# Threshold search of a sparse attention layer: where the candidate less the next bit is formed

## What is computed

```python
raw = jnp.einsum('bqhe,ble->bqhl', qi, ki).astype(f32) * IDX_DIM ** -0.5
score = jnp.einsum('bqhl,bqh->bql', jax.nn.relu(raw), wi.astype(f32)) * N_IDX_HEADS ** -0.5
score = jnp.where(adm[None], score, -jnp.inf)
_, idx = lax.top_k(score, topk)
```

## Time and profile before

| | us |
|---|---|
| median of three runs | 2905.49 |
| the profiled execution, device time | 2906.05 |
| its span in the trace | 2904.3 |
| TensorE busy in the span | 2825.2 (97%) |
| VectorE busy | 1538.2 (53%) |
| ScalarE busy | 700.3 (24%) |
| GpSimd busy | 899.6 (31%) |
| the search, first count to last candidate | 1456 to 1607.6 |

### The profile page before, as it was taken

How to read it: one execution, slowest core, us unless ns; L and a number is a source line. 1 busy time by engine, 2 the same in 40 slices (tenths; PEclk the granted TensorE clock), 3 DMA queues, 4 the chain that set the end, 5 groups by cost and what they waited for, 6 DMA issues and landing times. The chain is left out here.

```text
span 2904.3 us, 47791 instructions
## 1 busy us (share of the span) xinstructions
PE 2825.2 (97%) x18337; PEld 2662.8 (92%) x18337; DVE 1538.2 (53%) x2822; ACT 700.3 (24%) x1441; POOL 899.6 (31%) x854
## 2 busy tenths in 40 slices
PE   7999999999999999999978999999999999999998
PEld 6987799999999999998578777789999999999997
DVE  6146616544544444455688878533644454444455
ACT  4037711000000000013467766631100000000002
POOL 2233332222222222224024754323222222222221
PEclk9999999999999999999999999999999999999999
DMA  4530011111111111114012000021111111111112
GB/s 125 69 97 11 21 37 37 44 36 43 36 36 43 43 43 43 36 44 133 1 32 78 11 11 10 21 76 43 44 37 43 43 42 37 43 43 36 43 37 76
DMA packets 178206, 129.79 MB, mean 45 GB/s; under 512 B 25313, under 2 KB 168353, under 8 KB 177846
## 3 DMA queue, kind: packets, MB, share of 16 engines
q1 hardware_dynamic: 178066, 127.90, 15.4%
HBM read 111.13 MB, written 15.16 MB: 43 GB/s over the span
## 5 line engine op out<-in xcount | busy, mean ns | idle before, releaser
L1237 POOL CAST w_hi<-w_raw 128x1024 fp32r<-128x1024 f32 x120 | 145.1, 1209 | 1098.9 <-PE ps_gemm L1474 600.2
L684 DVE TENSOR_TENSOR h<-h,ps_gemm 128x1170 f32<-128x1170 f32 (+1 forms) x192 | 262.5, 1367 | 371.8 <-PE ps_gemm L1490 208.5
L1474 PE MATMUL ps_gemm<-xh,w_hi 128*128 128x390 f32 (+1 forms) x1920 | 445.8, 340 | 0.0
L1474 PE MATMUL ps_gemm<-xl,w_hi 128*128 128x390 f32 (+1 forms) x1920 | 444.9, 340 | 0.0
L1474 PE MATMUL ps_gemm<-xh,w_lo 128*128 128x390 f32 (+1 forms) x1920 | 444.7, 340 | 0.0
L1474 PEld LDWEIGHTS ps_gemm<-xh,w_hi 128*128 128x128 f32 x1920 | 349.2, 189 | 0.1
L1474 PEld LDWEIGHTS ps_gemm<-xl,w_hi 128*128 128x128 f32 x1920 | 348.1, 189 | 0.0
L1474 PEld LDWEIGHTS ps_gemm<-xh,w_lo 128*128 128x128 f32 x1920 | 348.0, 189 | 0.0
L1240 POOL TENSOR_TENSOR w_lo<-w_raw,w_hi 128x1024 fp32r<-128x1024 f32 x120 | 289.4, 2411 | 17.4
L692 ACT ACTIVATE ac<-ac 128x1184 f32<-128x1184 f32 x44 | 52.5, 1194 | 858.0 <-DVE ac L751 858.0
L1435 PE MATMUL ps_gemm<-xl,w_hi 128*128 128x390 f32 (+1 forms) x1056 | 246.6, 342 | 0.0
(11 more groups left out here) (418 smaller groups left out, 4672.6 us busy)
## 6 DMA issues: line engine op xcount, KB each, us to landing
w_raw<-in_w_gate SPq DMA_DIRECT2D x44, 512.0 KB, 3.8
w_raw<-in_w_up SPq DMA_DIRECT2D x44, 512.0 KB, 3.8
w_raw<-in_w_down SPq DMA_DIRECT2D x44, 512.0 KB, 3.4
w_raw<-in_w_in_b SPq DMA_DIRECT2D x13, 512.0 KB, 4.0
w_raw<-in_w_qkv_a SPq DMA_DIRECT2D x10, 512.0 KB, 4.0
residual_park<-h SPq DMA_DIRECT2D x1, 4680.0 KB, 13.7
h<-residual_park SPq DMA_DIRECT2D x8, 585.0 KB, 7.9
out<-yt SPq DMA_DIRECT2D x9, 512.0 KB
```

The lines of the kernel that those rows point to most:

```text
L684: dve.tensor_tensor(c3(h[:, m, :], l), c3(h[:, m, :], l), pse(j, l), ALU.add).then_inc(evac[j % 2], 1)
L1237: pool.tensor_copy(whi[c % 3][:], raw[c % 2][:]).then_inc(w_hi_done, 1)
L1474: mm = pe.matmul(ps[j % 2][:, m_, 0:ch], w[:, k, :], x[:, k, x0 + m_ * ch:x0 + (m_ + 1) * ch], start=(k == 0 and w is wh and x is XH), sto ...
```

## The change

ScalarE forms `above` behind its three counts of each round of the two loops, as a copy with a constant bias, into seven columns of `small` in SBUF. VectorE's subtraction L2503 is gone. VectorE waits for ScalarE's `above` between the comparison and the new candidate. The other edits follow from that: a semaphore more, one bit value less to set, fewer search steps to number.

```diff
         cand_new = sem("candidate_ready")
+        above_done = sem("candidate_less_next_bit_done")
...
+        above = small[:, 14:21]
...
             for n, (kind, j, view) in enumerate(steps):
                 counts(view, CAND[kind] + j, COUNTS[kind] + j)
+                if kind in ABOVE:
+                    act.activation(above, candm, ACT.Copy, bias=-2.0 ** (TOP[kind] - j - 1)).then_inc(above_done, 1)
                 if n in after:
                     take_projection(after[n])
...
-            sign, pred, tmp, need, bv = F(0), F(35), F(43), F(50), F(57, 6)
-            kk, above, bits_made = tb[0][:, 0:7], tb[0][:, 8:15], F(21)
+            sign, pred, tmp, need, bv = F(0), F(35), F(43), F(50), F(57, 5)
+            kk, bits_made = tb[0][:, 0:7], F(21)
...
                         wait_at(dve, cand_new, CAND[kind] + j, unroll, i)
-                        dve.tensor_scalar(above, candm, bv[:, j + 1:j + 2], None, ALU.subtract).then_inc(srch, 1)
                         counts(view, COUNTS[kind] + j, i, unroll)
                         dve.tensor_tensor(pred, cnt, kk, ALU.is_le).then_inc(srch, 1)
-                        wait_at(dve, srch, base + 2 * j + 2, 2 * unroll + 1, i)
+                        wait_at(dve, above_done, ABOVE[kind] + j + 1, unroll, i)
+                        wait_at(dve, srch, base + j + 1, unroll + 1, i)
                         dve.scalar_tensor_tensor(candm, pred, bv[:, j:j + 1], above, ALU.mult, ALU.add).then_inc(cand_new, 1)
```

More of the change, by code:

```diff
@@ L869, in build @@
         COUNTS = {"sign": 0, "high": 1, "above": 1 + S1, "low": 2 + S1}
-        SRCH_OPS = 1 + 3 + 6 + 2 + (1 + 3 * 11) + 1 + 1 + 2 + (1 + 4 * 9) + 2 + 1
+        ABOVE = {"high": 0, "low": S1}
+        TOP = {"high": S1 - 1, "low": S2 - 1}
+        SRCH_OPS = 1 + 3 + 6 + 2 + (1 + 3 * 6) + 1 + 1 + 2 + (1 + 4 * 5) + 2 + 1
         MASK_STEPS = [(6, k) for k in (0, 2, 3, 4, 5, 6, 7)] + [(c, k) for c in range(6) for k in range(8)]
@@ L2492, in bits @@
             def bits(view, kind, top, rounds, unroll):
-                for k in range(unroll + 1):
+                for k in range(unroll):
                     ins = dve.memset(bv[:, k:k + 1], 2.0 ** (top - k))
@@ L2509, in bits @@
                     dve.scalar_tensor_tensor(bv, bv, 2.0 ** -unroll, bv, ALU.mult, ALU.bypass).then_inc(srch, 1)
-                    wait_at(dve, srch, base + 2 * unroll + 1, 2 * unroll + 1, i)
-                step[0] += rounds * (2 * unroll + 1)
+                    wait_at(dve, srch, base + unroll + 1, unroll + 1, i)
+                step[0] += rounds * (unroll + 1)
                 dve.wait_ge(cand_new, CAND[kind] + rounds * unroll)
             flip(-1.0)
-            bits(high_half, "high", 14, 3, 5)
+            bits(high_half, "high", TOP["high"], 3, 5)
             high = F(0 + 43)
@@ L2526, in _ @@
             done(dve.tensor_tensor(kk, kk, cnt, ALU.subtract))
-            bits(low_kept, "low", 15, 4, 4)
+            bits(low_kept, "low", TOP["low"], 4, 4)
             done(dve.tensor_copy(bits_made.bitcast(I16)[:, 1::2], high))
```

## The result

The changed kernel took 2916.79 us (median of 6 runs, 2914.94 to 2921.59), the kernel before 2906.68 in the same comparison: ratio 1.0035, 95% interval 1.0025 to 1.0045, or about +10.2 us. It is slower, as forecast for 2912.2, but by more, and 0.8 us above the range's upper end. The profiled execution of after has a span of 2915.9 us.

The account below looks back on a forecast made before the run. TensorE's two long waits for the search were taken to bound the kernel. Saving -2.7 and ScalarE's operation +1.3 gave -1.4; with port +8.2 that made +6.8, taken as +6.7: 2912.2 us, range 2903.8 to 2916.0.

Parts of the forecast that it names:

- What bounds the kernel: TensorE, busy nearly always, waits twice for the search; the time changes by the sum of both waits' changes.
- the two waits: TensorE's two longest waits, inside the search: 15.3 and 18.6 us instead of 12.8 and 14.4.
- The port term: Candidates and `bv` updates with two SBUF operands wait for GpSimd: 3.0 and 5.2 us, sum +8.2.
- n = 18: That round's candidate misses GpSimd's second product by 0.2 us and doesn't wait; later by that, 2.2 us.
- n = 24: Its candidate misses GpSimd's second product by 0.2 us; the `bv` update behind it waits 2.1, before 1.9.
- The short ones: Candidates n = 5, 14 and 28 wait 0.4 us for GpSimd's cast; n = 9 waits 0.4 for a product.
- The saving: Without VectorE's subtraction an ordinary round saves 0.15 us: 1.2 before the kv copy, 1.5 behind job 8, together -2.7.
- ScalarE's operation: The new copy takes 0.18 us, hidden in rounds without a projection, 0.09 of the queue otherwise; sum +1.3 us.
- rival 3: Candidates n = 18 and 24 fall into GpSimd's second product, +2.2 us each: some 2916 us, chance 0.13.

Follow-up runs that it names:

- e6: The changed kernel without VectorE's wait for `cnt_done` ahead of the first two counts of a round: 2914.58 us, ratio 1.0019.
- e13: e3 without the `cnt_done` wait ahead of a round's first two counts, and with ScalarE's new operation issued twice: 2907.93 us, ratio 1.0006.
- e3: The changed kernel with the comparison's outcome in PSUM instead of SBUF: 2907.62 us, ratio 1.000.
- e2: The kernel before, VectorE still subtracting but writing `above` to SBUF instead of PSUM: 2923.10 us, ratio 1.0049.
- e8: The kernel before with the unread second input of the `bv` update in PSUM instead of SBUF: 2907.41 us, ratio 1.000.
- e11: e3 with the `cnt_done` wait ahead of the first two counts of a round written twice: 2913.78 us, ratio 1.002.
- e5: The kernel before without VectorE's wait for `cnt_done` ahead of the first two counts of a round: 2910.26 us, ratio 1.0005.

## Why the prediction was wrong, step by step

- **What bounds the kernel: right.** The time follows the two waits, 9.6 us against a measured 10.2 (7.3 to 13.1 by the interval).
- **The port term: right in kind and place, and nearly in size.** Before the kv copy 2.3 us (0.05 + 2.21 + 0.07 over the undisturbed durations) for 3.0; behind job 8, without n = 18, 4.6 us (0.22 + 1.87 + 0.16 + 0.17 + 2.14, of which the update behind n = 24 counts only by what it added) for 5.2. The short ones came out shorter because the candidates, having saved less, came later and met less of the cast. In e6, where they come earlier, the same ones take 0.54 (n = 5), 0.54 (n = 14) and 0.47 us (n = 28).
- **The saving: the term that was mis-sized.** The prediction took 0.05 us for a wait directly behind another, from the nearest gap, with 0 and 0.20 as bounds. It is 0.14 (e6 against after): 0.07 for the wait, and 0.07 for the register instruction in front of it, which the prediction did not count in an ordinary round. Of the 0.20 us between the subtraction and the first count, 0.16 stayed. A round saves 0.04 us in the high half and nothing in the low half, where a register instruction more stands ahead of the wait for `above`. Instead of -2.7 us the saving is some -0.3.
- **ScalarE's operation: right.** 0.194 us for 0.18, and 0.09 in the queue for 0.09 (e13). Since rounds stayed at 3.77, most of the +1.3 us wasn't paid. Saving and operation together were forecast at -1.4 us and are +0.7 in the waits of e3 (13.1 and 14.8).
- **n = 18: the step that failed.** The prediction put it clear of GpSimd's second product by 0.2 us and wrote that later by that it would wait 2.2. ScalarE starts its counts of n = 17 at a = 1547.44 in after. The product begins at a + 7.41, as forecast (7.4). But the candidates n = 17 and 18 come at a + 3.67 and a + 7.49 instead of 3.4 and 7.2. So n = 18 waited 2.1 us more. In e6 (a = 1546.99) they come at a + 3.50 and a + 7.31, and n = 18 gets by: the register instruction and the wait ahead of the first count make 0.17 to 0.18 of the 0.29 us, enough to decide it. That is the mechanism of rival 3, which forecast 2916 us with chance 0.13. Its other half, n = 24, did not fall in (0.23 us at 1582.58; the product began at 1582.65).

The trace of before would have shown n = 18 at risk. The round of n = 17 there (ScalarE's and VectorE's first count, the candidate n = 17, the product, the candidate n = 18):

```profile
1542.28 1.15 ACT L2164 ACTIVATE rl<-ki_old,small 128x1024 bf16<-128x1024 uint16 x1 [0.85 <-DVE small L2498]
1542.64 1.01 DVE L2460 TENSOR_SCALAR_CACHE_REDUCE ptb_h<-low_keep,small 128x768 bf16<-128x768 uint16 x1
1545.92 0.22 DVE L2507 SCALAR_TENSOR_TENSOR small<-small,ps_tr 128x7 f32<-128x7 f32 x1
1549.58 2.40 POOL L1208 TENSOR_TENSOR w_lo<-w_raw,w_hi 128x1024 fp32r<-128x1024 f32 x1
1549.72 0.22 DVE L2507 SCALAR_TENSOR_TENSOR small<-small,ps_tr 128x7 f32<-128x7 f32 x1
```

With a = 1542.28 the candidates come at a + 3.64 and a + 7.44, and n = 18 already lies 0.14 us behind the start of the product (a + 7.30). It took 0.22 us, with one tensor from SBUF and one from PSUM. The prediction's a + 3.4 is that of an ordinary round (a + 3.55 at n = 4) less 0.15 saved. But n = 17 begins a pass, as the only one of the nine rounds with a projection. Its first count starts 0.36 us behind ScalarE's instead of 0.27, and the prediction's own rule gives the first round of a pass no saving. With 3.64 in place of 3.4, and the prediction's 3.8 us to the next, n = 18 comes at a + 7.44, behind the product at a + 7.4. An estimate from the prediction's own terms is then +6.7 + 2.2 = +8.9 us.

The sum in its parts, forecast and measured: port 8.2 and 6.9, n = 18 nothing and 2.1, saving and ScalarE's operation -1.4 and +0.7; together +6.8, taken as +6.7, and +9.7. The parts that were off do not all go one way: the port term fell 1.3 us short, which took back part of the rest. Another 1.2 us of the distance to 2912.2 is the kernel before itself, whose median was 2906.68 in the comparison and 2905.49 in the three runs that the prediction started from. With a margin of 0.2 us, and bounds for the wait that were 0.20 apart, a chance of 0.13 for n = 18 falling in was too low.

## What to carry to other kernels

The time from one operation's start to the next one's is not what the first costs. Register instructions and waits stand between, take their own time, and stay when the operation goes: of 0.20 us only 0.04 went here. So look at every instruction between the two, and not only at those that the timeline lists. Where small operations share a port with long ones, count how many tenths each is away from the long one's start: a change of 0.1 us per round can cost 2 us at once, and one operand in PSUM instead of SBUF took it away here (e3). A margin no larger than the bounds of an unknown cost ahead of it is no margin. And take the place of a round from its own rows: the first round of a pass is not an ordinary one.

## What was not expected of the hardware

- A `tensor_scalar` of VectorE on 7 columns with input and output in SBUF waited for GpSimd as well (up to 2.39 us, five times over 1 us in e2); with its output in PSUM none of 31 did.
- The input that an operation bypasses counts as an operand: the `bv` update took up to 2.38 us with it in SBUF (after), and 0.16 with it in PSUM (e8).
- On VectorE a wait against a register's value takes 0.07 us though it is already satisfied (repeated in e11), and the register instruction in front of it another 0.07 (both taken out in e6: 0.14). Where an operation of 0.23 us starts just ahead of them, taking both out gains only 0.07 (e5).
- VectorE and GpSimd decide by hundredths of a microsecond: started 0.08 us ahead of the product an operation takes 0.23 us, and the product its usual 2.42; started 0.02 us behind, it takes 2.35 (e11). In the same hundredth it went either way: n = 31 at 1615.31 in after took 2.38 us, the `bv` update at 1485.70 in e3 took 0.17.
